# A GpSimd queue reordered in the first product of a PEER layer: gathers ahead of the weight tile's low half

## What is computed

```
expert, gate = top 16 of 16384 for each of 8 heads     (128 experts for each token)
act = gelu(w_down[expert] . x)
out = sum over experts of gate * act * w_up[expert]
```

## Time and profile before

| | before |
|---|---|
| median of 3 runs | 1537.17 us (1536.03 to 1537.38) |
| the profiled execution's own time | 1537.04 us |
| its span, first to last instruction | 1535.2 us |
| PE busy | 1520.1 us (99%) |
| DVE busy | 1158.4 us (75%) |
| POOL busy | 752.5 us (49%) |
| ACT busy | 637.0 us (41%) |
| mean granted TensorE clock | 0.998 |
| HBM traffic over the span | 271 GB/s |

### The profile page before, as it was taken

One profiled execution on the slowest core, in us unless ns is written; L12 is line 12 of the kernel. 1 busy time (PEld: TensorE's weight loads), 2 busy tenths in 40 slices (PEclk: granted clock), 3 DMA queues, 4 the chain that ended last, 5 costly groups with the idle time before them and its releaser, 6 DMA issues.

```text
span 1535.2 us, 23599 instructions
## 1 busy us (share of the span) xinstructions
PE 1520.1 (99%) x8616; PEld 1368.2 (89%) x8616; DVE 1158.4 (75%) x2407; ACT 637.0 (41%) x850; POOL 752.5 (49%) x469
## 2 busy tenths in 40 slices
PE   9999999999999999999999999999999999999997
PEld 8888899889899999999999999988888888888885
DVE  5563262477999979777878775888888888888787
ACT  4323244422234456546644673443333333333332
POOL 1553472224355887878787878622222223222230
PEclk9999999999999999999999999999999999999999
DMA  8622350333246999999899999999999999999981
GB/s 293 223 96 82 99 176 29 110 125 106 84 140 187 340 325 310 347 415 364 307 352 415 360 330 353 361 346 339 352 350 336 360 331 349 353 342 353 372 331 56
DMA packets 146254, 418.24 MB, mean 272 GB/s; under 512 B 18001, under 2 KB 52065, under 8 KB 145889
## 3 DMA queue, kind: packets, MB, share of 16 engines
q1 hardware_dynamic: 100648, 252.84, 47.5%
q0 software_dynamic: 39168, 142.62, 25.0%
q10 hardware_dynamic: 6328, 21.33, 3.5%
HBM read 371.36 MB, written 45.37 MB: 271 GB/s over the span
## 4 chain that ended last, share of the span: by engine, by line
PE 89%; DMA 6%; POOL 2%; DVE 1%; ACT 1%; issue 0%; SPq 0%; DVEq 0%; ACTq 0%
PE ps L1745 11%; PE ps L1747 11%; PE ps L1746 11%; PE ps L1312 9%; PE ps L1314 8%; PE ps L1313 8%; PE ps L429 6%; PE ps L431 6%; PE ps L430 6%; DMA raw<-in_down_t 3%; DMA act_d<-act_t 2%; POOL w_lo L1536 2%; PE ps L1167 1%; PE ps L1168 1%; PE ps L1169 1%; PE ps L1698 1%
## 5 line engine op out<-in xcount | busy, mean ns | idle before, releaser
L1575 ACT ACTIVATE w_hi<-raw 128x1024 fp32r<-128x1024 f32 x252 | 266.6, 1058 | 347.2 <-PE ps L1747 302.8
L1312 PE MATMUL ps<-b_hi,w_hi 128*128 128x368 f32 x1024 | 341.4, 333 | 2.1 <-ACT act_t L1581 2.1
L1313 PE MATMUL ps<-b_lo,w_hi 128*128 128x368 f32 x1024 | 336.5, 329 | 0.0
L1314 PE MATMUL ps<-b_hi,w_lo 128*128 128x368 f32 x1024 | 336.3, 328 | 0.0
L1536 POOL TENSOR_TENSOR w_lo<-raw,w_hi 128x1024 fp32r<-128x1024 f32 x119 | 287.3, 2416 | 72.7 <-ACT w_hi L1575 70.1
L1549 POOL DMA_INDIRECT rows<-in_w_up,expert x128 | 148.0, 1157 | 344.4 <-DVE ps L1867 332.0
L1747 PE MATMUL ps<-w_hi,b_lo 128*128 128x512 f32 x768 | 298.8, 389 | 0.0
L1746 PE MATMUL ps<-w_lo,b_hi 128*128 128x512 f32 x768 | 298.8, 389 | 0.0
L1745 PE MATMUL ps<-w_hi,b_hi 128*128 128x512 f32 x768 | 298.8, 389 | 0.0
L1788 DVE SCALAR_TENSOR_TENSOR rows<-rows,ps 128x1024 f32<-128x1024 f32 x144 | 174.3, 1219 | 81.0 <-DMA rows<-in_w_down,expert 65.9
L1874 DVE TENSOR_TENSOR w_lo<-raw,w_hi 128x1024 fp32r<-128x1024 f32 x133 | 162.8, 1224 | 69.7 <-ACT w_hi L1575 69.2
(11 more groups left out here) (293 smaller groups left out, 2505.3 us busy)
## 6 DMA issues: line engine op xcount, KB each, us to landing
raw<-in_down_t SPq DMA_DIRECT2D x128, 512.0 KB
raw<-in_up_t SPq DMA_DIRECT2D x128, 512.0 KB
raw<-in_units SPq DMA_DIRECT2D x75, 512.0 KB, 3.3
act_d<-act_t SPq DMA_DIRECT2D x124, 192.0 KB
c<-act_d SPq DMA_DIRECT2D x124, 192.0 KB
gate_d<-gmat ACTq DMA_DIRECT2D x32, 512.0 KB
v<-gate_d SPq DMA_DIRECT2D x16, 512.0 KB
i<-gate_d SPq DMA_DIRECT2D x16, 512.0 KB
```

Source lines behind the costliest of these rows:

```text
L1312: nc.tensor.matmul(out, ring.w_hi[:, s, w], b_hi[:, c, 0:T], start=c == 0, stop=False)
L1313: nc.tensor.matmul(out, ring.w_hi[:, s, w], b_lo[:, c, 0:T], start=False, stop=False)
L1314: last = nc.tensor.matmul(out, ring.w_lo[:, s, w], b_hi[:, c, 0:T], start=False, stop=c == KC - 1)
L1575: nc.scalar.activation(w_hi[:, u % W4, :], raw[:, u % W4, :], ACT.Copy).then_inc(hi_done, 1)
```

## The change

In each iteration of POOL's loop the gathers of the iteration, with the wait for `experts_ready` ahead of the first, now come first and the low half of tile `u+3` behind them.

```diff
             nc.gpsimd.memset(act_t[:, :, T:], GSCALE).then_inc(act_const, 1)
             for u in range(TILES):
-                if 0 < u < SPLIT_TILE:
-                    split_low(u + W4 - 1)
                 if u == LEAD:
                     pool.wait_ge(experts_ready, 1)
                 for r in range(NR):
                     if min(gathers[r], TILES - 1) == u:
                         gather(r)
+                if 0 < u < SPLIT_TILE:
+                    split_low(u + W4 - 1)
```

## The result

| | before | after |
|---|---|---|
| median of 20 runs each | 1536.87 us (1535.53 to 1538.97) | 1539.57 us (1538.05 to 1541.07) |
| the profiled execution's own time | 1537.04 us | 1539.53 us |
| its span | 1535.2 us | 1537.8 us |
| mean granted TensorE clock | 0.998 | 0.997 |

The ratio is 1.0016, with a 95% interval from 1.0010 to 1.0022: slower by 2.7 us. The forecast was 1542.1, slower by 5. The time lies in the range, and the sign is right. About half of the forecast loss is missing.

A forecast was written before the change was run, and what follows sets the result against it. PE was taken as the bound, busy in 1520.1 of 1535.2 us. 1537.04 + 4.0 (first gather) + 1.0 (gate stores) + 0 (end of low halves) = 1542.0, with 0.13 for the median 1542.1 us; range 1539.0 to 1546.5.

The forecast's parts named there:

- The place of the first gather: Tiles 14 and 15 of the first product: PE waits for late low halves, together 3.99 us lost, say 4.0.
- the 4 to 6 named as a sign of being right: Profile after: the first product ends 4 to 6 us later, the second takes as long as before.
- The wait for the indices: Tile 14's low half, now behind that wait and two gathers, ends at 495.42; PE loses 3.12 us.
- The tile after it: Tile 15's low half, behind two more gathers, ends at 500.21; PE waits 0.7 us more.
- The clock: PE idles 3.1 us ahead of tile 14; the clock was expected to stay up, so no loss counted.
- Rival 4: The clock falls to 1.2 GHz after the 3.1 us pause, up to +4.0 us, about 1546; chance 0.03.
- SP's queue: Tile 18's load and everything behind it on SP move later; costed at nothing, with 16 us of cover.
- the end of the low halves: At tile 120 the low half stands behind a gather waiting for DVE: bounds 0 and +0.9 us, taken as 0.
- The gate stores: Tiles 44 to 61 and 77 to 94: tile 53's low half 4.5 us later; +0.5 us per stretch, +1.0 in all.
- Rival 2: Earlier gathers leave fewer transfers competing with the `act_t` store; the 4.3 us lost there shrink, fully 1536.9; chance 0.14.
- The rule on queues that are served in turn: DMA engines serve queues in turn, so earlier gathers take turns from loads and stores; would make the sum larger.

The follow-up runs named there:

- Experiment 1: Kernel before with the gathers ahead of the low half in iteration 11 only: 1540.78 us, ratio 1.0023.
- experiment 10: The changed kernel, unaltered, profiled once more: 1539.28 us.
- experiment 6: Kernel before, but in iteration 11 the low half stands between its two gathers, behind the wait for the indices: 1540.49 us, ratio 1.0021.
- Experiment 4: Kernel before with gathers first only in the choosing tiles of the second and third block (44 to 60, 77 to 93): 1537.12 us, ratio 1.0000.
- experiment 2: Kernel before with gathers ahead of the low half only from iteration 28 on: 1534.32 us, ratio 0.9982.
- experiment 7: Kernel before with gathers first from iteration 28 on, and in the gate rounds each gather asked for one iteration sooner: 1540.43 us, ratio 1.0019.
- experiment 9: The changed kernel with the old order, low half first, in iteration 11: 1535.81 us, ratio 0.9989 against the kernel before.

## Why the prediction was right or wrong

**The sum.** Two errors of opposite sign partly cancel, so it is partly luck that the time lies well inside the range. The place of the first gather cost 4.64 us, forecast 3.99; from tile 44 on 2.09 us were won back where +1.0 was forecast. Without the 0.65 us of the first error the sum would be 1537.17 + 3.99 - 2.09 = 1539.07, at the lower bound of 1539.0. The first product ends 1004.04 - 1001.48 = 2.56 us later, outside the 4 to 6 named as a sign of being right.

**The wait for the indices: right.** Forecast 3.12 us, measured 2.97, ended by the low half of line 1536, with the gather at 490.63. Experiment 1 shows that it comes from iteration 11 and nothing else.

**The tile after it: right by itself, but it did not occur.** Forecast +0.87. Its low half ended at 500.12 (forecast 500.21). PE was slow enough not to need it.

**The clock: wrong.** "... so it fell only near the end of that window, after a pause longer than 3.1 us. I therefore count no clock loss." Rows 13 show a fall long after PE stopped, but PE never resumed there. I read the time until the fall as the pause needed for a fall. At tile 14 the clock fell at about 496.35, 3.7 us after PE's stop at 492.62, when PE had been back for 0.9 us: the effect came later than the pause lasted. And one profile is too few to read such a delay from: at the kernel's end the fall comes between 2.2 and 5.2 us after the last matmul in the twelve profiles. Rival 4, with a chance of 0.03, is what happened at this place, but smaller: the lower level lasted 3.4 us and cost 1.67, not 4.0, and it took away the second wait of 0.87. In sum the place cost 4.64 us, forecast 3.99.

**SP's queue and the end of the low halves: right, the first only just.** Tile 44 starts at 633.10, 4.64 us later than before, as much as tile 15: nothing between them was late. But the prediction gave SP's queue a cover of 16 us from the loads alone. It overlooked the eight copies and the store of tile 11 behind the load, whose cover was 0.47 us; in experiments 10 and 6 they cost 0.38 and 1.08. And the end of the low halves costs nothing: 0.01 to 0.03 us in four profiles of the new order.

**The gate stores: wrong in sign.** This is the larger error: +1.0 forecast, about -1.9 measured with the end of the loop. The step that failed is "Now it stands behind: 657.81 + 0.95 = 658.76, so 4.5 us later." It moves the low half and keeps the gather's wait where the trace of before has it. But that wait is for a dot product, the dot product waits for gathered rows, and those gathers had moved as well, one low half earlier in each iteration. The loop of gather and dot product is closed, and I shifted one link of it. I had used the very argument for the end of the low halves ("DVE may come to that dot product earlier than now") and not for tile 53. Experiment 4 comes nearest to the case that I worked out, a gather first with no head start from earlier tiles: the low half is 1.7 us late and PE loses 1.39 there. Even so the dot products are 2.95 us sooner, so the 4.5 us occur nowhere. With the head start the dot products run 4.0 us sooner (experiment 2), and the low half is 0.57 us late.

**Rival 2, "the rush thins out": its size fits, its mechanism is likely, not shown.** It is worth about half of its bound of 4.3 us. In the gate window the traffic is 414 or 415 GB/s wherever the low halves of the choosing tiles go first (six profiles), 398 to 407 wherever the gathers do. That by itself says only that the full rate ends sooner. The thinning is in the 58 us at the full rate: the queue of the gathers moves 7.4 to 7.7 MB there in the six profiles of the old order or half of it, 7.35 in experiment 4, and 7.0 to 7.1 in the five where the gathers go first from tile 28 on or earlier. That is about one gather of 0.5 MB less, and the waits for the store of `act_t` are 6.9 us instead of 11.1. My argument against it, "bytes and tiles stay the same", held for the whole kernel and not for the stretch. That the missing gather frees the stores is argued from these rows; no run removed bytes alone, and in three of the four profiles of the new order DVE, too, has 4 us less to do in the first window.

**The rule on queues that are served in turn** (the Trainium skill, DMA: Bandwidth & Descriptors, SWDGE vs HWDGE vs iDMA) would have made the sum larger. No run here shows the turns; the sum came out smaller, and in the rush the queue of the gathers moved less, not more (7.01 against 7.52 MB).

Open remain the clock's share in the medians, and whether the parts add up in the timed runs: experiments 1 and 2 give +3.5 and -3.0, together +0.5, the change +2.7, each with an uncertainty of about 1 us or more. By the medians the gates bring about 3 us (experiment 2), by the profiles 1.9.

## What to carry to other kernels

In an engine's queue, a wait holds all that stands behind it. So work that another engine needs on time belongs ahead of a long, one-time wait (here 6 us for the indices, which used up the whole cover), even if the same order is a gain in the steady state: keep the old order around the wait and the new one elsewhere, which here turned +2.7 us into -3.0. When you move a step that is part of a closed loop (gather, dot product, buffer free, gather), shift the whole loop before you read off who waits for whom. And look for a clock loss behind a pause as well as in it. Before you call a shifted operation covered, look at everything that stands behind it in each queue: here eight copies and a store behind one load.

## What the runs showed of the hardware that was not expected

TensorE's clock fell after a tile that started 2.97 us late (and at the same place in experiments 1 and 10) and after one that was 2.50 us late (experiment 7). In three of these four profiles PE was already at work again when it fell, in experiment 10 not yet; from PE's stop it took 2.3 to 3.7 us. At tile 14 it then stayed at 1.2 GHz for 3.4 us. It did not fall after tiles that were 1.97, 1.74 and 1.46 us late (experiments 7, 6 and 9). At the kernel's end, where PE stays idle, the granted clock is still 1.00 for 4.75 us after the last matmul in the kernel before, for 2.23 us in experiment 7 and for 5.15 us in experiment 1: one reading of this delay is no rule.

GpSimd's gathers cost its queue more than their 0.94 us when they come in a row: in experiment 9 they start 1.25 and 1.24 us apart, with 0.30 us of issue between them, and the four of them take from 490.25 to 495.10, 4.85 us, more than a tile of PE.
